# Moving the spectrum products behind the weight split in VectorE's mixer steps

## The reference

```python
def second_block(x, c, ctx, ...):                    # one layer
    h = modulate(rmsnorm_2(x, norm1_g), sh1, sc1)
    q, k, v, hv, hx1, hx2, gna, ghy = jnp.split(h @ w_in, IN_SPLITS, axis=-1)
    y_na = neighbourhood_attention(q, k, v, k_c, v_c, na_rpb)
    y_hy = hyena_mixer(hv, hx1, hx2, *hy_params)
    x = x + g1 * gated_merge(gna, ghy, y_na, y_hy, w_na_o, w_hy_o, w_out)
    ...

def hyena_mixer(hv, hx1, hx2, ...):
    u = short_conv(jnp.concatenate([hv, hx1, hx2], axis=-1), conv_w, conv_b)
    z, gates = parts[0], parts[1:]
    filt = hyena_filters(...)
    for n in range(HY_ORDER):                        # HY_ORDER = 2
        z = gates[n] * long_conv_bidir(z, filt[:, 0, n], filt[:, 1, n], bias[n])
    return z

def long_conv_bidir(u, h_fwd, h_bwd, bias):
    U = jnp.fft.rfft(u, n=2 * L, axis=1)
    K = jnp.fft.rfft(k2, n=2 * L, axis=0)
    return jnp.fft.irfft(U * K, n=2 * L, axis=1)[:, :L] + u * bias
```

## Time and profile before

| | before |
|---|---|
| time, median of 3 runs | 1028.42 us (1027.72 to 1030.04) |
| the profiled execution: time, span | 1028.42 us, 1026.6 us |
| TensorE matmul busy | 984.0 us (96%) |
| VectorE busy | 776.6 us (76%) |
| ScalarE busy | 504.2 us (49%) |
| GpSimd busy | 124.8 us (12%) |
| mean granted TensorE clock | 0.983 of full speed |

### The profile page before, as it was taken

The page is one execution under the profiler, slowest core; times in us unless marked ns, Lnnn a source line. Parts: engine busy times, 40 slices in busy tenths (PEclk is TensorE's granted clock), DMA queues, the critical chain, the costliest instruction groups (busy, mean ns, idle before and its releaser), DMA issues.

```text
span 1026.6 us, 20269 instructions
## 1 busy us (share of the span) xinstructions
PE 984.0 (96%) x7692; PEld 933.1 (91%) x7692; DVE 776.6 (76%) x1231; ACT 504.2 (49%) x740; POOL 124.8 (12%) x141
## 2 busy tenths in 40 slices
PE   5889999999999998999999999999999999999996
PEld 4369999999989988999999998989899999999995
DVE  6759888788866657989967675979676869876554
ACT  6345454344555544444544441476556565554441
POOL 4100000011100016500004500100000420000111
PEclk9599999999999999999999999999999999999999
DMA  8048777667743315566735632343434648654552
GB/s 234 1 159 289 268 251 267 207 231 257 252 145 123 127 63 184 200 230 225 266 113 198 221 125 116 129 149 124 144 134 129 224 177 285 230 191 151 169 190 76
DMA packets 38924, 186.26 MB, mean 181 GB/s; under 512 B 4984, under 2 KB 9625, under 8 KB 26010
## 3 DMA queue, kind: packets, MB, share of 16 engines
q1 hardware_dynamic: 38874, 185.57, 52.1%
HBM read 184.50 MB, written 1.05 MB: 181 GB/s over the span
## 4 chain that ended last, share of the span: by engine, by line
PE 86%; DVE 8%; ACT 3%; POOL 1%; issue 1%; DMA 0%; DVEq 0%; SPq 0%; ACTq 0%
PE ps L423 25%; PE ps L424 25%; PE ps L425 25%; DVE wl L364 2%; PE ps L1765 1%; PE ps L1984 1%; PE ps L2033 1%; PE ps L1809 1%; PE ps L2005 1%; DVE xl L1217 1%; ACT wh L358 1%; PE ps L1774 1%; PE ps L1827 1%; PE ps L1993 1%; PE ps L1783 1%
## 5 line engine op out<-in xcount | busy, mean ns | idle before, releaser
L423 PE MATMUL ps<-xh,wh 128*128 128x256 f32 (+3 forms) x1808 | 524.9, 290 | 8.7 <-DVE xl L1217 3.6
L424 PE MATMUL ps<-xh,wl 128*128 128x256 f32 (+3 forms) x1808 | 518.6, 287 | 0.0
L425 PE MATMUL ps<-xl,wh 128*128 128x256 f32 (+3 forms) x1808 | 516.8, 286 | 0.0
L364 DVE TENSOR_TENSOR wl<-stage,wh 128x1024 fp32r<-128x1024 f32 (+2 forms) x320 | 362.8, 1144 | 116.1 <-ACT wh L358 113.9
L358 ACT ACTIVATE wh<-stage 128x1024 fp32r<-128x1024 f32 (+2 forms) x320 | 306.5, 967 | 176.2 <-PE ps L425 141.2
L423 PEld LDWEIGHTS ps<-xh,wh 128*128 128x128 f32 x1808 | 343.1, 190 | 15.0 <-issue 5.4
L424 PEld LDWEIGHTS ps<-xh,wl 128*128 128x128 f32 x1808 | 342.6, 189 | 2.7 <-issue 1.2
L425 PEld LDWEIGHTS ps<-xl,wh 128*128 128x128 f32 x1808 | 341.3, 189 | 1.4
L423 PE MATMUL ps<-gh,wh 128*128 128x256 f32 (+1 forms) x528 | 150.3, 285 | 2.9 <-DVE wl L364 1.5
L424 PE MATMUL ps<-gh,wl 128*128 128x256 f32 (+1 forms) x528 | 149.6, 283 | 0.0
L425 PE MATMUL ps<-gl,wh 128*128 128x256 f32 (+1 forms) x528 | 149.1, 282 | 0.0
(11 more groups left out here) (247 smaller groups left out, 781.5 us busy)
## 6 DMA issues: line engine op xcount, KB each, us to landing
stage<-in_w_gu SPq DMA_DIRECT2D x66, 1024.0 KB, 4.8
stage<-in_w_dn SPq DMA_DIRECT2D x48, 704.0 KB, 4.1
adaw<-in_w_ada SPq DMA_DIRECT2D x48, 512.0 KB, 5.3
stage<-in_w_gates SPq DMA_DIRECT2D x8, 1024.0 KB, 4.8
stage<-in_w_hy SPq DMA_DIRECT2D x6, 1024.0 KB, 4.7
stage<-in_w_q SPq DMA_DIRECT2D x8, 512.0 KB, 4.7
stage<-in_w_k SPq DMA_DIRECT2D x8, 512.0 KB, 5.1
stage<-in_w_v SPq DMA_DIRECT2D x8, 512.0 KB, 5.1
```

The lines of the kernel that those rows point to most:

```text
L364: nc.vector.tensor_tensor(wl[:, b, w], stage[:, b, w], wh[:, b, w].bitcast(fp32), ALU.subtract).then_inc(split_lo, 1)
L423: nc.tensor.matmul(psum, wh[:, b, w], xhi, start=first and n == 0, stop=False)
L424: nc.tensor.matmul(psum, wl[:, b, w], xhi, start=False, stop=False)
L425: last = nc.tensor.matmul(psum, wh[:, b, w], xlo, start=False, stop=close and n == len(blocks) - 1)
```

## The change

In VectorE's program for the mixer, the two conditional blocks that issue `spectrum_product` and `product_folded` move from around `conv_sides` to behind `spectrum_joined`, and so behind `na_front`, `lo_part` and `na_out_lo` of the same step. The steps in which they are issued stay the same, as do all instructions, waits and semaphores.

```diff
             for n in range(MIXER_TILES):
                 if n and unit_scored(n - 1) is not None:
                     na_back(unit_scored(n - 1))
-                if n in PRODUCT_AT:
-                    spectrum_product(PRODUCT_AT.index(n))
                 if n < HY_TILES:
                     conv_sides(n)
-                if n in FOLDED_AT:
-                    product_folded(FOLDED_AT.index(n))
                 if n < 2:
                     for i in range(2):
                         rope_back(KN + 2 * n + i)
                 if unit_scored(n) is not None:
                     na_front(unit_scored(n))
                 lo_part(*four_ahead("hy", n))
                 if unit_attended(n) is not None and unit_attended(n) % 2:
                     na_out_lo(unit_attended(n) // 2)
                 if n in SPECTRUM_AT:
                     spectrum_joined(SPECTRUM_AT.index(n))
+                if n in PRODUCT_AT:
+                    spectrum_product(PRODUCT_AT.index(n))
+                if n in FOLDED_AT:
+                    product_folded(FOLDED_AT.index(n))
                 if n == 15:
                     for t in range(2):
                         second_signal(t)
```

## The result

| | before | after |
|---|---|---|
| time, median | 1028.42 us (5 runs, 1027.72 to 1031.43) | 1037.66 us (5 runs, 1035.02 to 1039.81) |
| ratio to before | 1 | 1.0078, 95% interval 1.0056 to 1.0098 |
| profiled execution: time, span | 1028.42, 1026.6 us | 1035.64, 1033.9 us |

The change makes the kernel slower, by 8.0 us if the ratio is taken (0.0078 x 1028.42). A second set of runs of the same kernel, beside other kernels, gave 1.0074 (1.0061 to 1.0088), 7.6 us. The forecast was 6.6 us.

A forecast was written before the change was run, and what follows sets the result against it. The prediction took TensorE's program to bound the kernel, with VectorE costing only where TensorE waits. Its terms, 1.95 + 1.66 + 0.35 + 2.68 = 6.64 us, added to 1028.42 gave 1035.1 us; range 1031.5 to 1038.0.

The forecast's parts named there:

- rival (c): The forecast waits plus one fall of TensorE's clock: 1036.8 us, or 1038.5 with a fall in each order; chance 0.13.
- the prediction's own sign of being wrong: Wrong if the clock's row shows 0.50 between 700 and 780 us; one of three such signs.
- Steps 9 to 11: VectorE idles before conv_sides(9), the attention chain is late, and TensorE loses 1.95 us at the transposes of step 13.
- Steps 12 and 13: The fold comes late behind the product and low halves; TensorE waits another 1.66 us at line 2042.
- Steps 18 to 20: The bias add of na_front(6) is 0.99 us late; the transposes of step 22 lose 0.35 us.
- Steps 21 to 23: The second fold comes late; TensorE waits 2.68 us for it at line 2055.
- The weight halves stay covered, nothing later swallows the loss: Late weight halves are for tiles four steps on, so cost nothing; nothing later has slack to swallow the loss.
- The clock: Any new TensorE wait might bring back half clock, 1.7 us per fall; the main forecast of 1035.1 us included none.
- Rival (a): The moved work stays hidden, since TensorE waited for almost nothing here: 1028.4 us; chance 0.07.
- Rival (b): Only the attention chain is late: about 1030.7 to 1033 us; chance 0.14.
- Rival (d): Faster, as lo_part before the product frees weight buffers earlier in steps 9 and 21: 1026.0 us; chance 0.04.
- the two bounds: Below, attention terms alone, 2.3 us, 1030.7 us; above, every VectorE idle stretch reaches TensorE whole, 9.8 us, 1038.3 us.

The follow-up runs named there:

- after_again: The full change once more, run beside three later kernels: 1036.81 us, ratio 1.0074 to the kernel before.
- after_dose: The full change with the multiplication of line 1634 done once more in step 12, in front of the product: 1038.91 us, ratio 1.0093.
- step 9 alone, filled: Kernel before with only step 9's product moved, and TensorE transposing the identity 16 times before step 13's transposes: 1031.10 us, ratio 1.0017.
- The dose: Line 1634's multiplication done once more in step 12, in the changed kernel (ratio 1.0093) and in the kernel before (1.0002).
- order0_only: Kernel before with the change in steps 9, 10, 12 and 13 alone: 1033.50 us, ratio 1.0038.
- products_only: Kernel before with only the four products moved behind lo_part, the folds staying behind conv_sides: 1035.56 us, ratio 1.0053.
- step9_only: Kernel before with only the product of step 9 moved behind lo_part: 1032.30 us, ratio 1.0027.
- order1_only: Kernel before with the change in steps 18, 19, 21 and 22 alone: 1034.73 us, ratio 1.0045.
- filled version: The change in steps 18, 19, 21 and 22 alone, with TensorE transposing the identity 22 times before line 2055's wait: 1032.82 us, ratio 1.0037.
- after_filled: The full change with TensorE transposing the identity into an unused part of bank 7 during three waits: 1035.48 us, ratio 1.0063.
- filled kernels: Full change, step 9's product alone, and steps 18 to 22 alone, each with identity transposes in TensorE's waits: ratios 1.0063, 1.0017, 1.0037.
- folds_only: Kernel before with only the four folds moved behind lo_part, the products staying at the front of their steps: 1028.69 us, ratio 0.9993.

## Why the prediction held, and where it fell short

The measured 1037.66 us lies in the range, 2.6 us above the forecast of 1035.1 and nearer to rival (c), one fall of the clock, at 1036.8. The waits were forecast rightly; the clock was not, and the prediction's own sign of being wrong, a clock row at 0.50 between 700 and 780 us, did appear (0.52 from 766.5 to 769.9). That the time still lies in the range is owed to the range, which took in rival (c), and in part to luck: the falls in step 14 of after_again and after_dose came where a late result hid them. Step by step:

- **Steps 9 to 11, 1.95 us at the transposes of step 13.** Right: TensorE's bracket says 2.05 us, and in the stage's time the transposes came 2.00 us late. The run with step 9 alone, filled, isolates it: 2.04 us.
- **Steps 12 and 13, 1.66 us at line 2042.** Right: 1.51 us in the bracket, 3.77 us for tiles 9 to 15 against a sum of 3.61. The dose shows that this queue leads straight to TensorE.
- **Steps 18 to 20, 0.35 us.** Right in place. TensorE's bracket shows 0.20 us; measured from tile 9 the transposes of step 22 start 4.13 us later than before (64.22 against 60.09), which is 0.36 us beyond the 3.77 us of order 0.
- **Steps 21 to 23, 2.68 us at line 2055.** Right: 2.60 us in the bracket. Without a fall of the clock tiles 18 to 27 took 3.05 us more, forecast 3.03.
- **The weight halves stay covered, nothing later swallows the loss.** Right: no new wait for `wl` in the stage, and order0_only keeps +3.8 us to tile 27.
- **The clock.** This is the term that was mis-sized. The forecast set it at nothing and gave one fall 0.13; the argument was that a single wait of 1.7 us did no harm before. The runs show that one wait of 2.05 us is enough in some executions (products_only, step9_only, after_again, after_dose) and not in others (order0_only, the first profile of the full change), and that 2.6 us was followed by a fall in both order1_only and that first profile, but not in after_again and after_dose. The wait of 1.7 us that ends at 837.2 before stands in all fourteen profiles and was followed by a fall in none; so the argument from it was right for its length and did not carry to the longer waits. A fall cost 1.5 to 1.6 us where no late result stood behind it, and 2.8 us where it lasted longer (43.85 against 41.02 in order1_only and its filled version). Rival (c), one fall, describes the stage of the first profile closely: waits of 6.8 us and a fall of 1.6 make the 8.42 us by which it is longer, against 6.64 + 1.7 = 8.34.

Rival (a), hidden work, holds for the folds alone. Rival (b), the attention chain alone, is excluded by the wait at line 2042 and the dose. Rival (d), earlier low halves, had nothing to act on: TensorE waited for none. Two readings in the prediction were loose without moving the forecast: the 2.2 us by which the folds were early holds for order 0 only (1.9 us in order 1), and the two bounds leave the clock out, so that (c) with two falls lies above the upper one.

Against the ratio's 7.6 to 8.0 us, the waits explain 6.8 (after_filled and after_again, profile), and after_filled's times give 6.5 us. The rest, about 1 us, fits a fall of the clock in a part of the executions. Where it fell is known for the profiled execution of each kernel alone, but the mean granted clock of every one is on record: 0.9791 over the eight of the full change against 0.9808 to 0.9813 over the three later sets of the kernel before. Within the 57 executions of those sets 0.001 of mean clock goes with 0.5 us, so the difference is worth 0.8 to 1.1 us (an estimate).

The Trainium skill ("TensorE: Matmul & The Clock Gate", Part 1) says that activity releases the throttle and its lack brings it back. The filled kernels agree as far as three profiles go: with transposes whose results nobody reads the clock stood at 1.00 over the same waits.

## What to carry to other kernels

Ask of every instruction that waits on an in-order engine what stands behind it, and whether the instruction in front of it is filling that very wait: here the three instructions of a product, which needed nothing in flight, covered a wait of about 2 us in step 9 and 2.6 us in the later steps (VectorE's idle of 1.86 and 2.62 us after the change), and behind the wait they became part of the chain. Count the slack of each result against the moment TensorE takes it, row by row; a busy share of 95% decided nothing, since 1.24 us more of VectorE's work was free in one order and cost 1.26 us in the other. And price a new wait of TensorE as long as the 2.05 and 2.6 us here with a possible fall of the clock behind it, unless another late result follows closely.

## What the hardware showed that I had not expected

A single idle stretch of TensorE of 2.05 us was followed by a fall of its clock in four profiled executions and not in two others, the full change among both. And two delays in series need not add: in after_again and after_dose TensorE ran at half the clock for 3.4 us of tile 14 at no cost in time (30.58 us for tiles 9 to 15 with the fall and without), since the vector work that TensorE needed next went on at its own speed.

The falls elsewhere differ between executions too. At the start of a feed-forward near 400 us the clock was low from 400.8 to 404.2 us before, and in folds_only, whose program is the same there, for twice as long:

```profile
398.30:405.10 6.80, 5.39 (x25) 5.10 (x26) 2.11 (x3) 1.79 (x2) 2.12 (x3) 0.52 0.72 270
```

The 29 executions of the kernel before that stood beside the last four kernels ran from 1027.07 us (mean clock 0.984) to 1031.84 us (0.981), with 0.978 for three of the ones above 1030.3; against that spread a change of 0.6 us cannot be told.
